# Value products ahead of the transposes in three attentions of a two-block transformer kernel

## The chip, the cores and the metric

The kernel runs on one core of a Trainium2 chip. The metric is the device time of one execution in microseconds (us). Matmuls run on TensorE (PE in the profile; PEld is its weight load), reductions and elementwise work on VectorE (DVE), activations and copies on ScalarE (ACT), a few small operations on GpSimd (POOL); SyncE (SP) issues the transfers. Each engine runs its own instructions in program order and waits for others on semaphores.

## What is computed

The reference runs two transformer blocks one after the other on x of 512 tokens by 1024 features, all in float32. Cut to the attentions:

```python
# block 1
proj = rms_norm(x) @ w_in
# A: 3 groups (window, dilation) = (128, 1), (512, 4), (2048, 16), 4 heads of 64 each
s = q @ k.T * 64 ** -0.5, masked to the window;  m = max(s);  p = exp(s - m);  l = sum(p)
o = (p / l) @ v;  lse = m + log(l);  the groups are weighed with softmax(lse)
# B (latent attention): 8 heads, queries and keys of 96, values of 64, no mask
p = softmax(q @ k.T * 96 ** -0.5);  o = p @ v
h = x + rms_norm(gates * (A @ w_o_a), gates * (B @ w_o_b), ... @ w_out);  h += mlp(h)
# block 2
# four mixers: S5, HGRN2, Fox, mLSTM.  C (Fox): 4 heads of 64, causal
s = q @ k.T * 0.125 + F_q - F_k, masked to k <= q;  p = softmax(s);  o = p @ v
h += rms_norm(mix @ w_out);  h += swiglu(h)
```

## The kernel before

The large products with weights take float32 operands split into a high and a low part and run as three matmuls each (`products`, L237 to L244). Weights come through a ring of three slots: a transfer fills `ring_raw`, ScalarE writes the high half (`split_hi`, L213), VectorE the low half (`split_lo`, L223).

All three attentions are one function, `stage_attention` (L705). It takes a list of tiles (`batches`) of 128 queries of one head:

- A has 24 tiles: 16 of the banded group (one query block against two or three key blocks) and 8 of the dilated ones (four separate 128 x 128 blocks in a tile). Beside it run the products of the two gates: `Beside.pe` issues one or two units of 12 matmuls in every round, directly behind the scores (L663); `Beside.act` adds the gate bias and makes high halves, `Beside.dve` low halves.
- B has 32 tiles, one query block against all 512 keys, and nothing beside it.
- C has 16 tiles, head by head with 1, 2, 3 and 4 key blocks (the causal part). Its scores are three matmul groups: q k, the gate rows (K = 4) and the mask. Beside it `Convolution` (L2211) puts work on VectorE in rounds 0 to 3 and 8 to 11 and four sigmoids on ScalarE in round 5.

The steps of tile i, each with its engine:

1. `scores(i)`, TensorE, L745, into bank i % 2.
2. Row maximum (L827) and `nm` = -scale * maximum (L829), VectorE.
3. `probs` = exp(scores + nm) with its row sum, ScalarE, L803; two buffers.
4. `turn(i)`, TensorE, L757: one transpose for each block of 128 columns, into bank 2 + i % 2. It waits for the exp of its tile (L751).
5. `evac(i)`: copy into `probsT` (L784 to L791, recorded as L629). Even tiles on ScalarE, odd tiles on VectorE.
6. `mix(i)`, TensorE, L769: probsT times the values, one product of 64 columns for each block, into bank 4 + i % 2. It waits for the copy of its tile (L763).
7. Division by the row sum into the output, VectorE, L841 and L844 or L847.

The order on each engine is written out by the loops. In round i ScalarE runs exp(i), then the copy of tile i - 1 if that is even, then the work beside (L795 to L810). VectorE runs the maximum of tile i, then the copy of tile i - 1 if that is odd, then the work beside, then the division of tile i - 2 (L821 to L849). TensorE runs the scores of tile i with the work beside, the transposes of tile i - 1, the value products of tile i - 2 (L774 to L782). At the end of A ScalarE takes the logarithm of the row sums (L814) and VectorE makes 24 subtractions (L854). Each attention is a block of its own: the next stage starts when all engines have ended it.

Of the kernel before, what the change touches and what calls it, by code (L numbers as in the profile page):

```python
# [627 lines left out]
def copy_out(k, who, dst, src):  # L628
    return k.nc.scalar.copy(dst, src) if who == "act" else k.nc.vector.tensor_copy(dst, src)  # L629
# [75 lines left out]
def stage_attention(k, batches, scale, bufs_kb, lse=None, beside=None):  # L705

    nc = k.nc
    nb = len(batches)  # L710
    scored, negmax, expd, turned, ev_act, ev_dve, mixed, out_free = (
        k.sig(n) for n in ("att_scored", "att_negmax", "att_exp", "att_turned", "att_ptT_act", "att_ptT_dve",
                           "att_mixed", "att_out"))
    k.att_n += 1
    probs = k.sb(f"probs{k.att_n}", bufs_kb, [P, 2, 512])
    probsT = k.sb(f"probsT{k.att_n}", bufs_kb + 4, [P, 2, 512])
    ns = max(len(b["segs"]) for b in batches)
    mx = k.sb(f"mx{k.att_n}", bufs_kb + 8, [P, nb, ns])
    nm = k.sb(f"nm{k.att_n}", bufs_kb + 8.5, [P, nb, ns])
    ls = k.sb(f"ls{k.att_n}", bufs_kb + 9, [P, nb, ns])  # L720
    li = k.sb(f"li{k.att_n}", bufs_kb + 9.5, [P, nb, ns])
    chain = k.sig("dve_chain")
    chain_act = k.sig("act_chain")

    def width(b):
        return b["segs"][-1][1]

    with nc.Block() as block:
        @block.sync
        def _(sp):  # L730
            if beside is not None:
                beside.sync(sp)

        @block.tensor
        def _(pe):
            def scores(i):
                b = batches[i]
                if i >= 2:

                    pe.wait_ge(expd.sem, expd.base + i - 1)  # L740
                for (c0, c1), parts in zip(b["segs"], b["scores"]):
                    for m, (a, r, lo, hi, *row) in enumerate(parts):

                        at = dict(tile_position=(row[0], 0)) if row else {}
                        mm = nc.tensor.matmul(k.pb[i % 2][:, lo:hi], a, r, start=m == 0,  # L745
                                              stop=m == len(parts) - 1, skip_group_check=True, **at)
                mm.then_inc(scored.sem, 1)

            def turn(i):
                b = batches[i]  # L750
                pe.wait_ge(expd.sem, expd.base + i + 1)  # L751
                if i >= 2:
                    ev = (ev_act, ev_dve)[i % 2]

                    pe.wait_ge(ev.sem, ev.base + i // 2)
                for c in range(0, width(b), P):
                    mm = nc.tensor.transpose(k.pb[2 + i % 2][:, c:c + P], probs[:, i % 2, c:c + P], k.ident[:, :])  # L757
                mm.then_inc(turned.sem, 1)

            def mix(i):  # L760
                b = batches[i]
                ev = (ev_act, ev_dve)[i % 2]
                pe.wait_ge(ev.sem, ev.base + i // 2 + 1)  # L763
                if i >= 2:

                    pe.wait_ge(out_free.sem, out_free.base + i - 1)
                for n, ((c0, c1), vs) in enumerate(zip(b["segs"], b["values"])):
                    for m, v in enumerate(vs):
                        mm = nc.tensor.matmul(k.pb[4 + i % 2][:, n * DH:(n + 1) * DH],  # L769
                                              probsT[:, i % 2, c0 + m * P:c0 + (m + 1) * P], v,  # L770
                                              start=m == 0, stop=m == len(vs) - 1, skip_group_check=True)
                mm.then_inc(mixed.sem, 1)

            for i in range(nb + 2):  # L774
                if i < nb:
                    scores(i)
                    if beside is not None:
                        beside.pe(pe, i)
                if 1 <= i <= nb:
                    turn(i - 1)  # L780
                if i >= 2:
                    mix(i - 2)  # L782

        def evac(who, eng, i):  # L784
            w = width(batches[i])

            eng.wait_ge(turned.sem, turned.base + i + 1)
            if i >= 2:
                eng.wait_ge(mixed.sem, mixed.base + i - 1)
            copy_out(k, who, probsT[:, i % 2, 0:w], k.pb[2 + i % 2][:, 0:w]).then_inc(  # L790
                (ev_act if who == "act" else ev_dve).sem, 1)  # L791

        @block.scalar
        def _(act):
            for i in range(nb + 1):  # L795
                if i < nb:
                    b = batches[i]
                    act.wait_ge(negmax.sem, negmax.base + i + 1)
                    if i >= 2:

                        act.wait_ge(turned.sem, turned.base + i - 1)
                    for n, (c0, c1) in enumerate(b["segs"]):
                        e = nc.scalar.activation(probs[:, i % 2, c0:c1], k.pb[i % 2][:, c0:c1], ACT.Exp,  # L803
                                                 bias=nm[:, i, n:n + 1], scale=scale,
                                                 accum_out=ls[:, i, n:n + 1])
                    e.then_inc(expd.sem, 1)
                if i >= 1 and (i - 1) % 2 == 0:
                    evac("act", act, i - 1)
                if beside is not None:
                    beside.act(act, i)  # L810
            if lse is not None:

                act.wait_ge(expd.sem, expd.base + nb)
                nc.scalar.activation(mx[:, :, :], ls[:, :, :], ACT.Ln).then_inc(chain_act.sem, 1)  # L814

        @block.vector
        def _(dve):
            link = Chain(dve, chain)
            if lse is not None:
                link(nc.vector.memset(ls[:, :, :], 1.0))  # L820
            for i in range(nb + 2):  # L821
                if i < nb:
                    b = batches[i]
                    m = len(b["segs"])
                    dve.wait_ge(scored.sem, scored.base + i + 1)
                    w = width(b)
                    link(nc.vector.tensor_reduce(  # L827
                        mx[:, i, 0:m], k.pb[i % 2][:, 0:w].rearrange("p (m w) -> p m w", m=m), AX.X, ALU.max))
                    nc.vector.tensor_scalar(nm[:, i, 0:m], mx[:, i, 0:m], -scale, None,  # L829
                                            ALU.mult).then_inc(negmax.sem, 1)  # L830
                if 1 <= i <= nb and (i - 1) % 2 == 1:
                    evac("dve", dve, i - 1)
                if beside is not None and i <= nb:
                    beside.dve(dve, i)
                if i >= 2:
                    j = i - 2
                    b = batches[j]
                    m = len(b["segs"])

                    dve.wait_ge(expd.sem, expd.base + j + 1)  # L840
                    link(nc.vector.reciprocal(li[:, j, 0:m], ls[:, j, 0:m]))  # L841
                    dve.wait_ge(mixed.sem, mixed.base + j + 1)
                    if m == 1:
                        nc.vector.tensor_scalar(b["out"], k.pb[4 + j % 2][:, 0:DH], li[:, j, 0:1], None,  # L844
                                                ALU.mult).then_inc(out_free.sem, 1)
                    else:
                        nc.vector.tensor_tensor(  # L847
                            b["out"], k.pb[4 + j % 2][:, 0:m * DH].rearrange("p (m e) -> p m e", m=m),
                            li[:, j, 0:m].unsqueeze(2).to_broadcast([P, m, DH]), ALU.mult).then_inc(out_free.sem, 1)  # L849
            if lse is not None:  # L850

                dve.wait_ge(chain_act.sem, chain_act.base + 1)
                for dst, i, n in lse:
                    nc.vector.tensor_tensor(dst, mx[:, i, 0:n], nm[:, i, 0:n], ALU.subtract)  # L854
                chain_act.base += 1
    for s in (scored, negmax, expd, turned, mixed, out_free):
        s.base += nb
    ev_act.base += (nb + 1) // 2
    ev_dve.base += nb // 2
    if beside is not None:  # L860
        beside.close()
# [2021 lines left out]
```

## Time and profile before

| | |
|---|---|
| time, median of 3 runs | 1804.71 us (1803.56 to 1804.91) |
| the profiled execution: its time / its span | 1806.47 us / 1804.6 us |
| TensorE busy / weight loads | 1625.3 us (90%) / 1303.4 us (72%) |
| VectorE / ScalarE / GpSimd busy | 827.6 us (46%) / 554.9 us (31%) / 260.4 us (14%) |
| mean granted TensorE clock | 0.911 of 2.4 GHz |
| HBM | 71 GB/s over the span |

The page cuts the span into 40 slices of 45 us; these two lines are the busy tenths of TensorE and its granted clock in tenths of full speed (9 is 90% or more).

```profile
PE   7987999668989899999998999399976899999997
PEclk9998999789999999999998999655568999999999
```

A lies in slices 5 to 8 (185 to 336 us), B in slices 10 and 11 (419 to 494 us), C in slices 27 and 28 (1173 to 1236 us). Matmul lengths in the timeline contain the pipeline's depth, so consecutive matmuls overlap; the distance from one start to the next is the rate. The number in square brackets at the end of a timeline row is the idle time of that engine ahead of it and what ended it.

### The profile page before, as it was taken

To read this page: it belongs to the slowest core of one execution; us is meant where nothing else is said; L and a number is where in the kernel's file an instruction comes from. 1 tells how busy PE (TensorE), PEld (TensorE's weight loads), DVE (VectorE), ACT (ScalarE), POOL (GpSimd) and SP (SyncE) were. 2 spreads that over 40 slices of the span, in tenths; PEclk is the share of its full clock that TensorE was granted. 3 is DMA by queue.
4 is the path that set the end of the run, shared out by engine and by line. 5 is a ranking of instruction groups with operands and counts; after the bars stand their busy time and mean duration, and the time that the engine had idled before them with its cause. 6 is when DMAs were issued, how large, how long until landed. Compare 5 with 4: busy or idle time off the path is not lost. (4 is left out here: it accounts for less than half of the span.)

```text
span 1804.6 us, 18401 instructions
## 1 busy us (share of the span) xinstructions
PE 1625.3 (90%) x7372; PEld 1303.4 (72%) x7372; DVE 827.6 (46%) x1217; ACT 554.9 (31%) x839; POOL 260.4 (14%) x275
## 2 busy tenths in 40 slices
PE   7987999668989899999998999399976899999997
PEld 6875777556767788888876667355775688888886
DVE  4233333456655444443454762463674543323334
ACT  4222333424443422232334212334122422212222
POOL 0000000000022795000011763000220200000000
PEclk9998999789999999999998999655568999999999
DMA  4322121220022222222222211100001123222222
GB/s 165 104 76 73 47 71 36 71 71 1 1 82 77 87 97 105 102 94 93 94 93 79 70 70 66 36 23 1 1 1 53 64 97 107 100 94 94 94 82 94
DMA packets 34633, 129.23 MB, mean 72 GB/s; under 512 B 4548, under 2 KB 18780, under 8 KB 22132
## 3 DMA queue, kind: packets, MB, share of 16 engines
q1 hardware_dynamic: 34260, 127.93, 20.6%
q8 instruction: 58, 0.95, 0.2%
q14 instruction: 27, 0.22, 0.0%
q10 hardware_dynamic: 288, 0.12, 0.0%
HBM read 124.82 MB, written 3.17 MB: 71 GB/s over the span
## 5 line engine op out<-in xcount | busy, mean ns | idle before, releaser
L223 DVE TENSOR_TENSOR ring_lo<-ring_raw,ring_hi 128x2048 fp32r<-128x2048 f32 (+5 forms) x115 | 267.7, 2331 | 246.3 <-ACT ring_hi L213 246.2
L242 PE MATMUL bank<-xT_hi,ring_hi 128*128 128x512 f32 (+1 forms) x864 | 343.7, 398 | 5.1 <-PEq L1257 3.4
L242 PE MATMUL bank<-xT_hi,ring_lo 128*128 128x512 f32 (+1 forms) x864 | 340.0, 393 | 0.0
L242 PE MATMUL bank<-xT_lo,ring_hi 128*128 128x512 f32 (+1 forms) x864 | 339.8, 393 | 0.0
L213 ACT CAST ring_hi<-ring_raw 128x2048 fp32r<-128x2048 f32 (+5 forms) x115 | 213.0, 1854 | 274.7 <-DMA ring_raw<-in_w_ff 130.8
L242 PEld LDWEIGHTS bank<-xT_hi,ring_hi 128*128 128x128 f32 (+1 forms) x864 | 164.0, 190 | 45.1 <-issue 10.0
L242 PEld LDWEIGHTS bank<-xT_hi,ring_lo 128*128 128x128 f32 (+1 forms) x864 | 163.3, 189 | 35.9
L242 PEld LDWEIGHTS bank<-xT_lo,ring_hi 128*128 128x128 f32 (+1 forms) x864 | 163.8, 190 | 34.3
L242 PE MATMUL bank<-ring_hi,hid_hi 128*128 128x512 f32 x432 | 169.9, 393 | 3.8 <-DVE ring_lo L223 3.8
L242 PE MATMUL bank<-ring_lo,hid_hi 128*128 128x512 f32 x432 | 169.4, 392 | 0.0
L242 PE MATMUL bank<-ring_hi,hid_lo 128*128 128x512 f32 x432 | 169.2, 392 | 0.0
L1131 POOL TENSOR_TENSOR stat<-stat 128x1 f32<-128x1 f32 x28 | 18.3, 654 | 700.8 <-DVE stat L1172 700.8
L242 PE MATMUL bank<-ring_hi,xT_hi 128*128 128x512 f32 (+1 forms) x288 | 111.2, 386 | 9.0 <-DVE ring_lo L223 9.0
L242 PE MATMUL bank<-ring_lo,xT_hi 128*128 128x512 f32 (+1 forms) x288 | 110.2, 383 | 0.0
L242 PE MATMUL bank<-ring_hi,xT_lo 128*128 128x512 f32 (+1 forms) x288 | 110.0, 382 | 0.0
L242 PEld LDWEIGHTS bank<-ring_hi,hid_hi 128*128 128x128 f32 x432 | 82.0, 190 | 21.3 <-DVE ring_lo L223 4.2
L803 ACT ACTIVATE probs<-bank,nm 128x128 f32<-128x128 f32 (+3 forms) x96 | 50.3, 528 | 149.1 <-DVE nm L829 149.0
L242 PEld LDWEIGHTS bank<-ring_hi,hid_lo 128*128 128x128 f32 x432 | 81.9, 190 | 17.2
L242 PEld LDWEIGHTS bank<-ring_lo,hid_hi 128*128 128x128 f32 x432 | 81.9, 190 | 17.0
L242 PEld LDWEIGHTS bank<-ring_hi,xT_hi 128*128 128x128 f32 x288 | 58.9, 204 | 21.7 <-issue 6.4
L827 DVE TENSOR_REDUCE mx<-bank 128x1 f32<-128x512 f32 (+4 forms) x72 | 43.3, 601 | 54.3 <-PE bank L745 54.3
L242 PEld LDWEIGHTS bank<-ring_hi,xT_lo 128*128 128x128 f32 x288 | 58.8, 204 | 9.1
(440 smaller groups left out, 2305.1 us busy)
## 6 DMA issues: line engine op xcount, KB each, us to landing
ring_raw<-in_w_ff SPq DMA_DIRECT2D x32, 1024.0 KB, 4.9
ring_raw<-in_w_up SPq DMA_DIRECT2D x22, 1024.0 KB, 4.9
ring_raw<-in_w_proj SPq DMA_DIRECT2D x8, 1024.0 KB, 5.1
ring_raw<-in_w_gates SPq DMA_DIRECT2D x8, 1024.0 KB, 4.9
ring_raw<-in_w_out SPq DMA_DIRECT2D x8, 1024.0 KB, 4.9
ring_raw<-in_w_fm SPq DMA_DIRECT2D x12, 512.0 KB, 4.3
ring_raw<-in_w_dn_a SPq DMA_DIRECT2D x6, 1024.0 KB, 4.9
ring_raw<-in_w_proj SPq DMA_DIRECT2D x8, 512.0 KB, 4.6
```

The source lines that it names most:

```text
L213: k.nc.scalar.copy(k.ring.hi[:, g % SLOTS, 0:n], k.raw[:, g % SLOTS, 0:n]).then_inc(k.w_hi.sem, 1)
L223: k.nc.vector.tensor_tensor(k.ring.lo[:, g % SLOTS, 0:n], k.raw[:, g % SLOTS, 0:n], plain(k.ring.hi[:, g % SLOTS, 0:n]), ALU.subtract).the ...
L242: mm = k.nc.tensor.matmul(out, x, y, start=first and n == 0, stop=last and n == 3 * len(pairs) - 1)
L803: e = nc.scalar.activation(probs[:, i % 2, c0:c1], k.pb[i % 2][:, c0:c1], ACT.Exp, bias=nm[:, i, n:n + 1], scale=scale, accum_out=ls[:, i, ...
L827: link(nc.vector.tensor_reduce(mx[:, i, 0:m], k.pb[i % 2][:, 0:w].rearrange("p (m w) -> p m w", m=m), AX.X, ALU.max))
L1131: g.tensor_tensor(self.rs[:, x:x + 1], self.ms[:, 16 + x:17 + x], self.half, ALU.pow).then_inc(self.root.sem, 1)
```

## The change

Two statements of TensorE's loop change places. In every round TensorE issues the value products of tile i - 2 directly behind the scores of tile i (and the products beside them), and the transposes of tile i - 1 behind those. Each step keeps its own wait. The instructions of all engines are the same in number and kind, and the order on the other engines is not touched. It applies to A, B and C alike.

```diff
                     scores(i)
                     if beside is not None:
                         beside.pe(pe, i)
+                if i >= 2:
+                    mix(i - 2)
                 if 1 <= i <= nb:
                     turn(i - 1)
-                if i >= 2:
-                    mix(i - 2)
```

## Rows read from the trace of the kernel before

**Rows 1.** The page's first part: busy time of each engine.

```profile
PE 1625.3 (90%) x7372; PEld 1303.4 (72%) x7372; DVE 827.6 (46%) x1217; ACT 554.9 (31%) x839; POOL 260.4 (14%) x275
```

**Rows 2.** Stretches: us, busy PE, PEld, DVE, ACT, POOL (x), PEclk, DMA, GB/s.

```profile
185.00:336.00 151.00, 148.55 (x745) 116.18 (x744) 49.34 (x115) 53.55 (x136) 0.00 (x0) 0.98 0.15 53
419.00:494.00 75.00, 72.27 (x461) 54.80 (x462) 48.60 (x146) 33.26 (x82) 0.00 (x0) 1.00 0.01 1
1173.00:1236.00 63.00, 57.55 (x185) 37.62 (x185) 34.57 (x98) 18.05 (x47) 0.00 (x0) 0.54 0.04 17
196.00:199.80 3.80, 3.80 (x18) 3.14 (x17) 0.00 (x0) 0.63 (x2) 0.00 (x0) 1.00 0.00 0
419.00:424.00 5.00, 3.50 (x12) 1.70 (x13) 1.92 (x5) 2.04 (x5) 0.00 (x0) 1.00 0.00 0
294.00:297.00 3.00, 3.00 (x8) 2.32 (x7) 1.76 (x6) 1.22 (x7) 0.00 (x0) 0.50 0.00 0
```

**Rows 3.** Timeline of attention B: start us, length us, engine, line, tiles [idle before].

```profile
429.47 1.08 PE L745 MATMUL bank<-kTb,qTb 96*128 96x512 f32 x2
...
430.39 0.60 PE L757 MATMUL bank<-ident,probs 128*128 128x128 f32 x4
430.59 0.69 DVE L827 TENSOR_REDUCE mx<-bank 128x1 f32<-128x512 f32 x1 [0.31 <-PE bank L745]
...
430.83 1.00 PE L769 MATMUL bank<-vB,probsT 128*128 128x64 f32 x8
...
431.50 0.69 ACT L803 ACTIVATE probs<-bank,nm 128x512 f32<-128x512 f32 x1 [1.41 <-DVE nm L829]
...
431.67 1.08 PE L745 MATMUL bank<-kTb,qTb 96*128 96x512 f32 x2
...
432.09 0.19 ACT L803 ACTIVATION_READ_ACCUMULATOR probs<-bank,nm 128x1 f32 x1
432.18 0.58 ACT L629 COPY probsT<-bank 128x512 f32<-128x512 f32 x1
432.33 0.61 PEld L757 LDWEIGHTS bank<-ident,probs 128*128 128x128 f32 x4 [0.42 <-ACT probs L803]
...
433.58 0.69 DVE L629 COPY probsT<-bank 128x512 f32<-128x512 f32 x1
...
433.86 1.08 PE L745 MATMUL bank<-kTb,qTb 96*128 96x512 f32 x2
...
434.38 0.28 DVE L844 TENSOR_SCALAR oB<-bank,li 128x64 f32<-128x64 f32 x1
```

**Rows 4.** Timeline, the end of attention B.

```profile
486.50 1.08 PE L745 MATMUL bank<-kTb,qTb 96*128 96x512 f32 x2
...
492.01 0.28 DVE L844 TENSOR_SCALAR oB<-bank,li 128x64 f32<-128x64 f32 x1 [0.61 <-PE bank L769]
```

**Rows 5.** Timeline, the end of attention A.

```profile
330.47 0.60 PE L757 MATMUL bank<-ident,probs 128*128 128x128 f32 x4
...
331.11 0.59 ACT L629 COPY probsT<-bank 128x512 f32<-128x512 f32 x1 [3.54 <-PE bank L757]
...
334.25 1.76 DVE L223 TENSOR_TENSOR ring_lo<-ring_raw,ring_hi 128x1536 fp32r<-128x1536 f32 x1 [1.17 <-ACT ring_hi L213]
```

**Rows 6.** Timeline of attention C: round 4, and its last rounds.

```profile
1187.55 0.47 ACT L629 COPY probsT<-bank 128x384 f32<-128x384 f32 x1
1187.70 1.12 PE L757 MATMUL bank<-ident,probs 128*128 128x128 f32 x4 [1.21 <-ACT probs L803]
...
1188.61 1.38 PE L769 MATMUL bank<-tm,probsT 128*128 128x64 f32 x6
...
1230.47 0.47 ACT L629 COPY probsT<-bank 128x384 f32<-128x384 f32 x1
...
1231.53 3.09 PE L769 MATMUL bank<-tm,probsT 128*128 128x64 f32 x14
...
1234.73 0.28 DVE L844 TENSOR_SCALAR ycat<-bank,li 128x64 f32<-128x64 f32 x1 [1.00 <-PE bank L769]
```

## The prediction, made blind

> **What bounds the kernel now.** The first part of the page shows TensorE busy for 1625.3 us of a span of 1804.6 us [rows 1]. The profiled execution took 1806.47 us, so 1.87 us lie around the span. The median of the timed runs is 1804.71 us, 1.76 us below this execution; I make the sum on the execution and then carry it to the median. The table by stretch [rows 2] puts the three attentions at 151, 75 and 63 us, with TensorE busy for 148.6, 72.3 and 57.6 us. They are therefore near TensorE's own rate, but at different clocks: the banded and dilated attention (below A) at 0.98, the latent one (B) at 1.00, that is 2.4 GHz, and Fox (C) at 0.54, nearly all of it 1.2 GHz. In A every round also holds 12 or 24 gate products. B has nothing beside it, C has a convolution on VectorE and ScalarE.
>
> I write S, T, V for the scores, transposes and value products of a tile, and E for the copy of transposed probabilities into probsT. Now TensorE runs S(i), T(i-1), V(i-2); after the change S(i), V(i-2), T(i-1). The same instructions are issued, without a new buffer or a DMA. Two waits change places. T(i-1) waits for exp(i-1), and now gets V's time more. V(i-2) waits for E(i-2), and loses the cover of T(i-1). What counts is where E stands in its engine's order: for even tiles E(i-2) is on ScalarE *behind exp(i-1)*; for odd tiles it is on VectorE and follows T(i-2), which would now end just before S(i).
>
> **B, steady rounds.** The timeline of two rounds [rows 3] gives the period: S of tile 5 (26 rounds before tile 31 at 486.50 [rows 4]) starts at 429.47, S of even tile 6 at 431.67, S of tile 7 at 433.86, so a pair takes 4.39 us. Starts give the parts: S to T 0.92, T to V 0.44, V to S 0.84, sum 2.20 each. TensorE's weight load for T had waited 0.42 us for exp and started at 432.33, 0.05 after the accumulator read ended (432.28); the matmul array itself was hardly idle, as the scores still ran. So exp and TensorE end together now, and the gain to be had in B is small: T takes 0.44 for 512 columns in one go, S has two matmuls of 512, so S alone would need about 0.85 (an estimate) of the 0.92, and no more than 0.07 a round can be won.
>
> Then the odd tile's chain, from S(odd) = 0: reduction at 1.12 (430.59), exp at 2.03 (431.50), accumulator read ends at 2.81, E of the tile before at 2.71 to 3.29 (432.18 + 0.58). Now this E ends behind T and V and nobody notices. After the change V(even) needs it, right behind S(even).
> - V(odd) in the round of S(odd): T(odd) starts 0.44 before S(odd). E on ScalarE follows the start of such a T by 0.64 (330.47 to 331.11 [rows 5]); I take that for VectorE too. E runs 0.20 to 0.89 (0.69 by 433.58). The weight load can start at 0.94. It would anyway have started near 0.7, so the loss is small: V at 1.04 with 0.1 for the first weight load, T(even) at 1.88, S(even) at 2.32.
> - VectorE's bookkeeping behind E (the division starts 0.80 after E, lasts 0.28; the next can start 0.2 after it) ends at 1.20 instead of being long over at 1.12, so reduction, exp and the ScalarE copy come 0.08 later: E(even) ends at 3.37.
> - V(even): 3.37 + 0.05 for the release + 0.1 for the first load = 3.52; + 0.84 for V and 0.44 for T: the next S(odd) at 4.80.
> A pair goes from 4.39 to 4.80, or +0.41. Bounds: with neither first load nor VectorE's delay, 3.29 + 0.05 + 0.84 + 0.44 = 4.62 (+0.23); with 0.25 for the load (432.33 to 432.58) and 0.2 for the delay, 5.07 (+0.68). I take +0.41, since a load that finds the array idle has nothing to wait for, unlike that of 432.33. Rounds 3 to 31 are 14 pairs: **+5.7 us** (3.2 to 9.5). At the start of the stage TensorE waits for exp(0) and exp(1) in both orders, nothing.
>
> **B, its end.** The last S starts at 486.50, the last division at 492.01, 5.51 later [rows 4]. After: V(30) at 3.52, T(31) at 4.36, E(31) on VectorE 5.00 to 5.69, V(31) at 5.84 for 1.00, the division at 6.94: **+1.4 us** (1.2 to 1.7). The cover that is gone is V(30), under which E(31) now runs.
>
> **A.** Between S(i) and V(i-2) lie 12 gate products or more; at full clock 17 of them take 3.8 us [rows 2], so that is at least 2.7 us. E(i-2) hides under them. T(i-1) comes up to 0.84 us later (V's length), and with it, on ScalarE, E, the gate biases and the high halves of the weight ring, on VectorE the low halves; all of these run ahead of TensorE, which is busy for 148.6 of 151 us [rows 2], so nothing until the end. There T(22) starts at 330.47 and E(22) at 331.11; the biases and the high half on ScalarE, then the low half on VectorE (334.25) and its last divisions and subtractions follow in order and end the stage [rows 5]. V(21) now stands ahead of T(22): **+0.84 us** (0, if the chain had slack; 1.7, if TensorE's own end decides, whose E(22) and E(23) are now uncovered). After two rounds of dilated scores the clock drops for over 3 us: in 294 to 297 it was 0.50 [rows 2], that is 1.2 GHz, and half of such a stretch, some 1.7 us, is lost each time. V, T and S remain one run of small products between the same gate products, so I take no change, but one more or fewer of either kind of round may fall: from -3.4 (both gone) to +5.1 (three more).
>
> **C.** At half the clock S takes, by B's 0.85, some 1.7 us for four blocks and 0.85 for two, and has two smaller products behind it; that covers E(odd). E(even) arrives in time in the rounds whose exp is not late. In round 4 it is: E(2) is 1187.55 to 1188.02, T(3) started at 1187.70 after 1.21 us of waiting [rows 6]. V(2) would start at 1188.02 + 0.05 + 0.2 (the first load at half the clock) = 1188.27, with T behind it instead of ahead: **+0.5 us** (0.3 to 0.7; round 2 loses some 0.2 in the same way, which the later exp(3) hides). In rounds 8 and 12 E(even) ends shortly ahead of the scores: 0, at most 0.2 each. At the end V(14) waits for E(14), which ends at 1230.94: V at 1231.2, T(15) 6 products of 0.22 (3.09 / 14) later at 1232.5, E(15) after 0.91 (1187.70 to 1188.61) and 0.2 at 1233.6 to 1234.3, V(15) at 1234.6 for 1.8, the division at 1236.6, against 1234.73: **+1.9 us** (1.5 to 2.2). Sum of C +2.4 (1.8 to 3.3).
>
> **Sum.** 5.7 + 1.4 + 0.84 + 2.4 = 10.3. On the execution 1806.5 + 10.3 = 1816.8; from the median, 1804.7 + 10.3 = **1815.0**.
>
> **Rivals.**
> 1. *The exp wait was the dearer one; faster.* If E(even) could end before S(even) does, B would go at TensorE's own rate, -0.07 x 28 = -2.0, and C would keep the 1.21 of round 4, and with the ends hidden too: 1804.7 - 2.0 - 1.2 = 1801.5, and about 1800.5 with the like in C's round 2. It decides from the point at which E(even) ends before 2.32 + 0.7 = 3.0 after S(odd); the rows put it at 3.29. Speaks for it: TensorE's load does wait for exp in each round. Chance 4%.
> 2. *Only the ends cost.* If a pair in B stays within 0.1 of 4.39, since both waits fall in time that the array uses: 1.4 + 0.84 + 2.4 + 0 to 1.4 = 4.6 to 6, that is 1809 to 1811; with C's also smaller, 1807. Chance 11%.
> 3. *The clock of B falls.* TensorE would be idle 0.4 us of 4.8. At 1.2 GHz a pair takes 2 x 4.27 = 8.5 us, +3.7 over 4.80; all 14 pairs +52 (1867), a few pairs +5 to +20. Against it: in 419 to 424 TensorE was busy for 3.50 of 5.00 us and the clock stayed at 1.00 [rows 2]; for it: C was at 0.50 with TensorE nearly filled. Chance 6%. The Trainium skill, "TensorE: Matmul & The Clock Gate", section "A second HAM failure mode: psum-queue depth-cycling", speaks against this change: short idle gaps between groups of matmuls, it says, made the clock of another kernel swing between its two levels. By that rule B would end at the times of this rival; the row of 419 to 424 has larger gaps at the full level, so the trace does not agree so far.
> 4. *The change does nothing*, as the scheduler of the engine would order the work by itself: TensorE's rows are in the program's order, under 1%, 1804.7.
>
> **How the numbers follow.** My forecast has 78%: 1815.0, and its own terms end at 1808 and 1822 without all extremes together (all low 1807.5, all high 1826). Range 1808 to 1822: it holds most of the forecast and the upper half of rival 2; rival 3 and rival 1 are left out. A measurement can tell about 0.2%, 3.6 us, from no change. Faster 0.03 (rival 1), same 0.07 (the rest of it, 4 and the low part of 2), slower 0.90.
>
> **What would show it.** In B: a pair of S starts 4.80 apart (4.6 to 5.1), TensorE's waits for ACT and DVE copies probsT in place of those for probs, no wait of T for exp; the last division 6.9 behind the last S. In A the same length but 0.8 more behind the last gate product, no waits inside. In C one wait of V(2), a longer end. B unchanged in the steady rounds would make the forecast wrong, as would a granted clock below 1.00 there; A's clock dips could hide some us of either sign.

## The result and the profile after

The changed kernel takes 1817.28 us (median of 4 runs, 1816.4 to 1819.2) against 1804.81 us for the one before (median of 4, 1803.56 to 1808.32): 12.5 us slower, a ratio of 1.007 with a 95% interval of 1.0058 to 1.0082. The profiled execution took 1816.96 us, its span is 1815.2 us, against 1806.47 and 1804.6 before. The forecast was 1815.0 with a range of 1808 to 1822.

The page of after, its busy times and the granted clock in 40 slices:

```profile
PE 1633.3 (90%) x7372; PEld 1299.2 (72%) x7372; DVE 825.2 (45%) x1217; ACT 555.1 (31%) x839; POOL 259.7 (14%) x275
...
PEclk9998999779999999999998999655567999999999
```

TensorE has the same 7372 instructions as in [rows 1], and the busy times of VectorE, ScalarE and GpSimd are within 2.4 us of those before. TensorE's row is 8.0 us longer, but it doesn't tell where: the modelled lengths of its matmuls also cover most of its short waits (67.28 of 68.00 us in B's rounds, shown below), and they grow where the clock is lower. Where the time arose is read by marking the same instruction in both timelines; the difference of the two starts is how far the changed kernel is behind there:

| instruction | before, us | after, us | behind by |
|---|---|---|---|
| A, first scores | 185.8 | 186.1 | +0.3 |
| A, last mask product | 324.9 | 323.1 | -1.7 |
| A, the 24 subtractions | 337.0 | 336.1 | -0.9 |
| B, first scores | 419.6 | 417.2 | -2.4 |
| B, last scores | 486.5 | 489.9 | +3.4 |
| B, last division | 492.0 | 497.7 | +5.7 |
| gate sigmoids, table load behind B | 496.7 | 503.6 | +6.9 |
| C, first scores | 1174.5 | 1181.7 | +7.2 |
| C, last division | 1234.7 | 1245.0 | +10.3 |
| end of the span | 1804.6 | 1815.2 | +10.5 |

B's rounds cost 5.8 us, its end 2.3, the stage behind it 1.2, C 3.1. A came out shorter, because two clock dips of before (one is in [rows 2], 294 to 297; the other, at 0.50 too, lies in 311 to 314) are absent in this execution. Another 1.5 us were won between A's subtractions and B's first scores, in work whose order was not changed.

**B, one pair of rounds.** Timeline of after (start us, length us, engine, line, tiles, idle before and its releaser), to be laid beside [rows 3]:

```profile
427.55 1.02 PE L745 MATMUL bank<-kTb,qTb 96*128 96x512 f32 x2
...
427.75 0.69 DVE L629 COPY probsT<-bank 128x512 f32<-128x512 f32 x1 [0.72 <-PE bank L757]
...
428.50 0.97 PEld L769 LDWEIGHTS bank<-vB,probsT 128*128 128x128 f32 x8 [0.75 <-DVE probsT L629]
...
428.75 0.68 DVE L827 TENSOR_REDUCE mx<-bank 128x1 f32<-128x512 f32 x1
...
429.44 0.61 PE L757 MATMUL bank<-ident,probs 128*128 128x128 f32 x4
...
429.65 0.69 ACT L803 ACTIVATE probs<-bank,nm 128x512 f32<-128x512 f32 x1 [1.80 <-DVE nm L829]
...
429.88 1.02 PE L745 MATMUL bank<-kTb,qTb 96*128 96x512 f32 x2
...
430.33 0.58 ACT L629 COPY probsT<-bank 128x512 f32<-128x512 f32 x1
...
430.96 0.97 PEld L769 LDWEIGHTS bank<-vB,probsT 128*128 128x128 f32 x8 [0.88 <-ACT probsT L629]
...
431.90 0.61 PE L757 MATMUL bank<-ident,probs 128*128 128x128 f32 x4
...
432.35 1.02 PE L745 MATMUL bank<-kTb,qTb 96*128 96x512 f32 x2
```

From the scores of an odd tile at 427.55: VectorE's copy starts 0.20 later, the weight load of the value products 0.95, the next reduction 1.20, the transposes 1.89, exp 2.10, ScalarE's copy ends 3.36 (430.33 + 0.58), the transposes follow at 4.35 and the next odd scores at 4.80. Both value products wait for their copy (0.75 and 0.88 us on the weight-load row), and no transposes of these rounds wait for exp.

**A.** What TensorE waited for between 185 and 337 us (total, times, longest), and the place of the last line:

```profile
PE bank L769 <- DVE probsT L629: 0.8, 1, 0.8
PE bank L745 <- PEq L886: 0.7, 1, 0.7
PE bank L769 <- ACT probsT L629: 0.7, 1, 0.7
PE bank L242 <- ACT gates L1398: 0.4, 1, 0.4
```

```profile
250.28 0.48 ACT L629 COPY probsT<-bank 128x384 f32<-128x384 f32 x1 [3.77 <-PE bank L757]
...
250.65 0.69 ACT L1398 ACTIVATE gates<-bank,cols 128x512 f32<-128x512 f32 x1
...
251.49 0.47 PE L242 MATMUL bank<-xT_hi,ring_hi 128*128 128x512 f32 x1 [0.41 <-ACT gates L1398]
```

The first and third line are the two copies of A's end. The last was not foreseen. The gate bias (L1398) frees the PSUM bank of a gate product. It stands on ScalarE behind the copy, and the copy comes later by the length of the value products. The gate product at 251.49 waited for it 0.41 us and started 0.15 after it ended. By the starts of the rounds, A's rounds 6 and 12 took 0.26 and 0.63 us longer than before.

**B, its end**, in the timeline of after:

```profile
489.88 1.02 PE L745 MATMUL bank<-kTb,qTb 96*128 96x512 f32 x2
...
493.28 1.10 PE L769 MATMUL bank<-vB,probsT 128*128 128x64 f32 x8 [0.91 <-ACT probsT L629]
...
494.87 0.69 DVE L629 COPY probsT<-bank 128x512 f32<-128x512 f32 x1 [2.54 <-PE bank L757]
...
495.62 1.93 PE L769 MATMUL bank<-vB,probsT 128*128 128x64 f32 x8 [0.78 <-DVE probsT L629]
...
497.66 0.28 DVE L844 TENSOR_SCALAR oB<-bank,li 128x64 f32<-128x64 f32 x1 [1.64 <-PE bank L769]
```

The value products of tile 30 wait for ScalarE's copy and those of tile 31 for VectorE's; the last eight take 1.93 us in place of 1.00. The table by stretch (us, busy PE, PEld, DVE, ACT, POOL, granted clock, DMA, GB/s) shows a lower clock there:

```profile
424.00:492.00 68.00, 67.28 (x403) 45.18 (x403) 42.79 (x130) 28.49 (x71) 0.00 (x0) 1.00 0.00 1
492.00:495.00 3.00, 1.92 (x16) 1.44 (x14) 0.43 (x3) 1.23 (x3) 0.00 (x0) 1.00 0.02 5
495.00:498.00 3.00, 1.93 (x8) 1.74 (x8) 1.27 (x5) 0.00 (x0) 0.00 (x0) 0.62 0.00 0
498.00:501.00 3.00, 2.74 (x13) 2.77 (x14) 0.82 (x2) 1.20 (x2) 0.00 (x0) 0.50 0.01 3
```

During the 68 us of B's rounds the clock stays at 1.00 in spite of the gaps. From 492 on TensorE is busy for 1.92 of 3.00 us, and within 495 to 498 the clock falls to 0.50, that is 1.2 GHz. The transposes of the next stage run at that level as well (16 of them take 3.65 us in place of 1.94). The busy share alone does not explain the fall. The kernel before has stretches as empty there, at the full level:

```profile
492.00:495.00 3.00, 1.94 (x16) 1.73 (x16) 1.36 (x3) 1.71 (x4) 0.00 (x0) 1.00 0.01 3
495.00:498.00 3.00, 1.27 (x6) 1.09 (x7) 1.41 (x3) 1.66 (x3) 0.00 (x0) 1.00 0.00 0
```

### The profile page after: what moved, and what is told of

It reads as the page before. It is cut to its first block and busy times, and to the rows that moved or that the text cites. A ratio compares the mean times of both kernels' runs of the same rounds, so it can differ in the third digit from the quotient of the medians.

```text
span 1815.2 us, 18401 instructions
## 1 busy us (share of the span) xinstructions
PE 1633.3 (90%) x7372; PEld 1299.2 (72%) x7372; DVE 825.2 (45%) x1217; ACT 555.1 (31%) x839; POOL 259.7 (14%) x275
```

## The experiments

All comparisons are with the kernel before, run beside each kernel on the same chip; 1 permille is 1.8 us. Where one difference in us is given with a ratio, it is worked out from the ratio. What is read from a trace is read from one execution.

### One attention at a time

```diff
+                early = k.att_n in (1,)      # A; (2,) for B, (3,) for C
+                if early and i >= 2:
+                    mix(i - 2)
                 if 1 <= i <= nb:
                     turn(i - 1)
-                if i >= 2:
+                if not early and i >= 2:
                     mix(i - 2)
```

A alone:

> The changed order in A alone, B and C as before. Account of the prediction, mended by the trace of after: the copies, and the gate biases behind them on ScalarE, come later by the length of the value products, and TensorE waits for a gate bank in two rounds (0.3 and 0.6 us) and ends 0.9 later: +1.8 us, less or more by 1.7 for each clock dip that comes or goes (the profiled execution of before had two, that of after none), so the median between -1.5 and +3. Rival (the loss of the whole change is spread over all three attentions by the lost cover): +4, a third of 12.5.

Measured: 1807.14 against 1804.46 us, ratio 1.0013 (1.0005 to 1.0022), +2.3 us. From A's first scores to its last mask product it took 137.1 us, against 136.0 in the C-alone kernel, which has the old order in A and no clock dip there either; from there to the subtractions 13.0 against 12.1. So A costs 1.1 us in its rounds and 0.9 at its end. That these add up to nearly the +2.3 is no proof, for more moved in this execution where the order is as before: against the C-alone kernel 1.3 us were won between A and B, and 2.8 were lost between C and the end of the span.

B alone:

> The changed order in B alone. Account of the prediction: the pair of rounds takes 4.79 instead of 4.39 us, 14 pairs, +5.7; end of the stage +1.4 to +2.3; the transposes behind it at a lower clock up to +1.2: +8 to +9 us in all. Rival (spread evenly): +4.

Measured: 1815.91 us, ratio 1.0061 (1.0047 to 1.0075), +11.0 us: more than expected. In its trace B is 7.5 us longer from the first scores to the last division, the stage behind it 1.2, and the products behind that another 1.5, for the clock is at 0.50 until past 506 us.

C alone:

> The changed order in C alone. Account of the prediction: +2.4 to +3 us, of which 0.5 in round 4 and 1.9 at the end. Rival (spread evenly): +4; rival (C is limited by TensorE at the low clock, the order plays no part): 0.

Measured: 1807.93 us, ratio 1.0017 (1.0008 to 1.0026), +3.1 us, and 3.1 us from C's first scores to its last division in the trace. TensorE's waits in C:

```profile
PE bank L769 <- ACT probsT L629: 3.7, 3, 1.8
...
PE bank L769 <- DVE probsT L629: 0.8, 1, 0.8
```

That is the start, round 4 and the end. But the rounds between, in which nothing waits, were each 0.10 to 0.11 us longer than before, ten times in a row. First a round of C alone, then the same round of the kernel before:

```profile
1220.94 1.91 PE L769 MATMUL bank<-tm,probsT 128*128 128x64 f32 x8
...
1222.65 0.42 PE L757 MATMUL bank<-ident,probs 128*128 128x128 f32 x1
...
1222.99 0.50 PEld L745 LDWEIGHTS bank<-fm 64*128 64x128 f32 x2 [0.22 <-issue]
```

```profile
1220.73 0.42 PE L757 MATMUL bank<-ident,probs 128*128 128x128 f32 x1
...
1220.94 1.81 PE L769 MATMUL bank<-tm,probsT 128*128 128x64 f32 x8
...
1222.68 0.50 PEld L745 LDWEIGHTS bank<-fm 64*128 64x128 f32 x2
```

The scores' first weight load now stands behind the transposes, and the row shows it 0.22 us idle ("issue": it waited for nothing in the profile); it comes 0.34 us after the transposes' start. Before, the value products followed a one-block transpose by 0.21, and the scores' load came behind the value products without idle time ahead of it. So in C the order costs a little by itself.

Taken one at a time the three come to 16.4 us, together the change costs 12.5. The sum of three such intervals is wide (some 4 us), and the clock took another course behind the stages from kernel to kernel; the runs don't settle how the difference of 3.9 us divides between the two.

### Is it the copy's place behind exp?

The changed order in B alone, and on ScalarE:

```diff
             for i in range(nb + 1):
+                if k.att_n == 2 and i >= 1 and (i - 1) % 2 == 0:
+                    evac("act", act, i - 1)
                 if i < nb:
...
-                if i >= 1 and (i - 1) % 2 == 0:
+                if k.att_n != 2 and i >= 1 and (i - 1) % 2 == 0:
                     evac("act", act, i - 1)
```

> The changed order in B alone, and there ScalarE copies the even tile before the exp of the next instead of behind it. Account of the prediction (the copy is late because it stands behind exp): the copy ends 0.84 after the scores start, a pair takes 2.33 + 2.22 = 4.55 instead of 4.79, 3.4 us less than with the changed order alone, about +3.5 to +4.5 against before. Rival (what is lost is the cover of the transposes, wherever the copy stands): pair 4.79, the same time as with the changed order alone.

Measured: 1812.9 against 1804.46 us, ratio 1.0041 (1.0028 to 1.0054), +7.4 by the ratio and +8.4 by the medians: 3.0 (medians) to 3.6 us (ratios) less than B alone. The timeline:

```profile
440.93 1.02 PE L745 MATMUL bank<-kTb,qTb 96*128 96x512 f32 x2
...
441.13 0.59 ACT L629 COPY probsT<-bank 128x512 f32<-128x512 f32 x1 [2.00 <-PE bank L757]
441.61 0.69 ACT L808 ACTIVATE probs<-bank,nm 128x512 f32<-128x512 f32 x1
441.76 0.97 PEld L769 LDWEIGHTS bank<-vB,probsT 128*128 128x128 f32 x8 [0.64 <-ACT probsT L629]
...
442.90 0.69 ACT L808 ACTIVATE probs<-bank,nm 128x512 f32<-128x512 f32 x1 [0.51 <-DVE nm L834]
...
443.15 1.02 PE L745 MATMUL bank<-kTb,qTb 96*128 96x512 f32 x2
...
444.10 0.97 PEld L769 LDWEIGHTS bank<-vB,probsT 128*128 128x128 f32 x8 [0.75 <-DVE probsT L629]
```

The copy starts 0.20 after the scores instead of 2.78 behind those of the odd tile, with exp behind it. The weight load of the value products starts 0.83 after the scores in this round and 0.95 in the other; the starts of the scores (440.93, 443.15, 445.48) make a pair of 4.55, as worked out. The rival's 4.79 is out. About 60% of the steady loss (0.25 of 0.41 a pair) is the place of ScalarE's copy behind exp; the rest is that a copy right behind its transposes has only the scores as cover (with a whole round of cover, in the version without the waits below, no such wait is left). The level was above the expectation again, as with B alone. In the trace 3.0 us lie behind B's last division, where the clock was at 0.50 for some 10 us.

### What B's end costs

```diff
-                early = k.att_n in (2,)              # B alone
+                early = k.att_n == 2 and i < nb       # b_old_end: rounds 2 to 31 only
+                early = k.att_n == 2 and i >= nb      # b_new_end: round 32 only
```

> The changed order in B alone and only in its rounds 2 to 31; in round 32 the transposes of tile 31 stand ahead of the value products of tile 30, as before. Theory: of the 11.5 us that the changed order in B alone costs, 5.7 are the steady rounds and the rest comes from the end, where TensorE waits twice for a copy and its clock then falls to 1.2 GHz and stays there for 6 to 10 us. So here +5.5 to +6.5 us, and the clock at 1.00 up to 20 us behind the last division. Rival (the clock falls because of the idle gaps in all rounds of B): the clock falls here as well, +9 or more.

Measured: 1811.02 against 1805.1 us, ratio 1.0035 (1.0023 to 1.0048), +5.9 by the medians and +6.3 by the ratio. In the trace B is 5.8 us longer from first scores to last division, and behind it (last division at 495.5) the clock stays up:

```profile
492.00:495.00 3.00, 2.56 (x22) 2.27 (x21) 1.48 (x7) 1.25 (x3) 0.00 (x0) 1.00 0.02 5
495.00:498.00 3.00, 2.28 (x20) 2.02 (x19) 0.85 (x2) 1.19 (x3) 0.00 (x0) 1.00 0.01 3
498.00:501.00 3.00, 0.84 (x4) 0.67 (x4) 1.92 (x4) 1.67 (x3) 0.00 (x0) 1.00 0.00 0
```

> The converse: B as before up to round 31, and only in round 32 the value products of tile 30 ahead of the transposes of tile 31. Theory: about +1.5 by the two uncovered copies and another +2 to +4 by the clock behind them: +3.5 to +5.5 us, the granted clock at 0.5 within 3 us of the last division. Rival (idle gaps in all rounds of B bring the clock down): +1.5, clock at 1.00.

Measured: 1808.61 us, ratio 1.0019 (1.001 to 1.0028), +3.5 by the medians and +3.4 by the ratio, with B's rounds as before. Here the last division is at 493.4; the clock falls about 2 us ahead of it and returns nearly 7 us later:

```profile
489.00:492.00 3.00, 2.22 (x15) 1.98 (x16) 1.11 (x4) 0.00 (x0) 0.00 (x0) 0.85 0.00 0
492.00:495.00 3.00, 2.28 (x11) 2.12 (x12) 0.28 (x1) 0.00 (x0) 0.00 (x0) 0.50 0.00 0
495.00:498.00 3.00, 2.64 (x13) 2.24 (x11) 1.93 (x3) 2.11 (x4) 0.00 (x0) 0.52 0.01 3
498.00:501.00 3.00, 1.68 (x7) 1.43 (x8) 0.84 (x2) 1.98 (x3) 0.00 (x0) 1.00 0.00 0
```

In the trace 2.2 us are lost up to the last division and another 1.2 in the stage behind it. The two runs add up to 9.7 of B's 11.0 us by the ratios, 9.4 of 11.5 by the medians. One instruction group moved in one round of 34 costs more than a quarter of the change (3.5 of 12.5; the interval of the 3.5 is 1.8 to 5.1). The rival, that the idle gaps in all rounds bring the clock down, is out as far as one traced execution can tell: they are all there in the first of these kernels, and the clock did not fall.

### A version without the waits

```diff
+                lag = 3 if k.att_n in (2, 3) else 2
+                if lag == 3 and 3 <= i:
+                    mix(i - 3)
                 if 1 <= i <= nb:
                     turn(i - 1)
-                if i >= 2:
+                if lag == 2 and 2 <= i < nb + 2:
                     mix(i - 2)
...
-                if i >= 2:
-                    j = i - 2
+                if i >= lag:
+                    j = i - lag
```

with one round more in the loops of TensorE and VectorE.

> In B and C the value products of THREE tiles back stand directly behind the scores and ahead of the transposes of the last tile, and VectorE divides tile i - 3 in round i; A as before. The same buffers. Account of the prediction: each copy has a whole round of cover and exp has that of the value products, so no wait is left in the steady rounds of B: a pair takes 4.27 to 4.30 instead of 4.39, -1.5 us; C wins 0.5 of round 4's wait; the ends cost nothing. 1802.5 against 1804.5, which lies at the edge of what can be told. Rival (putting the value products behind the scores costs by itself, as 64-column products cannot hide the next weight load): +2 to +6.

Measured: 1807.99 against 1805.1 us, ratio 1.0017 (1.0008 to 1.0026), +2.9 by the medians and +3.1 by the ratio: a miss in sign. The mechanism was right in B, where the value products of two rounds apart start

```profile
440.17 1.00 PE L769 MATMUL bank<-vB,probsT 128*128 128x64 f32 x8
...
444.46 1.00 PE L769 MATMUL bank<-vB,probsT 128*128 128x64 f32 x8
```

so a pair takes 4.29 us, and from first scores to last division 1.7 us are won. But the clock fell within 495 to 501 us, and the 1.7 us were gone by C. C was 0.7 us longer. And 2.6 us more were lost between C's last division and the end of the span, where the clock was at 0.50 for longer (on average 0.70 in 1370 to 1380 us against 1.00 before). With B alone in this order:

> Value products of three tiles back directly behind the scores in B alone; A and C as before. With B and C both so, the profiled execution won 1.6 us from B's first scores to its last division (pair 4.29 instead of 4.39), and the whole kernel still came out 2.9 us slower. Theory: part of that was C, where value products behind the scores cost 0.1 us in each round by themselves, and part the granted clock behind B and behind C, which falls at other places when the stages ahead take another time. So here B is 1.6 shorter again and the kernel between 1802.5 and 1806. Rival (the order in B itself hurts what follows, by the clock behind it): 1807 or more.

Measured: 1804.64 against 1804.21 us, ratio 1.0003 (0.9994 to 1.0012): no difference. In the trace B won 1.7 us again, the clock averaged 0.67 and 0.76 in 492 to 495 and 495 to 498, and at C's first scores the kernel was as far ahead as at B's. B's own gain is paid back behind it.

This also limits what the end of B shows. TensorE's one wait there is 0.34 us in this kernel, and yet the clock fell. Where it fell in the traces sorts the kernels into three. In the four with the changed order in B's last round (after, B alone, the copy ahead of exp, the end alone) it fell 0.6 to 2.3 us ahead of the last division. In the two with value products of three tiles back it fell 5 us behind it. In four with the old order there it did not fall (before, C alone, the old end, and the kernel with the gate bias first, told below). But in the fifth of these, A alone, it fell 6 us behind the last division, with the same instructions in B and behind it as in the kernel before (the row of 498 to 501 in its trace):

```profile
498.00:501.00 3.00, 3.00 (x8) 2.31 (x7) 1.22 (x2) 3.00 (x7) 0.00 (x0) 0.50 0.01 3
```

So a fall in the stages behind B needs no change in B. The early fall came with the changed last round in each of four traces and in none of the other seven; what in that order brings it, and whether it needs the waits for the copies, stays open.

### The gate bank in A

The order of A changed, and on ScalarE:

```diff
+                if k.att_n == 1:
+                    beside.act(act, i)
                 if i >= 1 and (i - 1) % 2 == 0:
                     evac("act", act, i - 1)
-                if beside is not None:
+                if beside is not None and k.att_n != 1:
                     beside.act(act, i)
```

> The changed order in A alone, and there ScalarE does the gate biases and the high halves of the ring ahead of the copy of the even tile. Theory: in the changed order TensorE waits for a gate bank in two rounds because the bias that frees it stands behind a later copy; with the bias first these two waits (0.3 and 0.6 us) go, A's first 16 rounds are 0.9 shorter than with the changed order alone. The end may be some us longer, since the last copy now stands behind a high half. Rival (the gate bank is late for another reason): the waits stay.

Measured: 1804.05 against 1805.1 us, ratio 0.9995 (0.9987 to 1.0004): no difference from the kernel before. TensorE's waits in A are now

```profile
PE bank L769 <- DVE probsT L629: 0.8, 1, 0.8
...
PE bank L769 <- ACT probsT L629: 0.7, 1, 0.7
```

with no line for the gates, and first scores to last mask product take 136.2 us, against 137.1 with the changed order alone. That is the expected 0.9, and within 0.2 of what the old order takes without clock dips (136.0). The end of A, which might have been longer, took 12.7 us against 13.0. By the ratios the kernel is 3.2 us faster than A alone, and only 1.2 of that lie in A; the rest is not explained. It is the best kernel that has the changed order anywhere, and it doesn't beat the one before by what can be told.

## Why the prediction was right, and where it was off

The sign, the mechanism and the range held; the time was 2.3 us (of 12.5) short. On the profiled execution the forecast was 1816.8 and the measured time 1816.96, and that close hit is luck. The terms named below cost some 14.3 us in that trace, 4.0 more than the 10.3 of the sum. The absent dips of A (3.2) and the 1.5 us between A and B hid this.

- **B's rounds** (predicted +5.7, pair 4.80): the pair is 4.80, and the 14 pairs cost 5.7; round 2 adds 0.1. 66.9 us from the scores of tile 0 to those of tile 31 became 72.7, +5.8, and the same with the old end. The steps lie within 0.03 us of those worked out, with one exception in which two errors cancel: the value products started with their weight load (0.95 and 3.41 after the odd scores, not 1.04 and 3.52) and then took 0.94 to the transposes and not 0.84. That the copy's place behind exp matters was tested by moving it.
- **B's end** (predicted +1.4): 2.3 us in after, 2.2 when the end alone is changed. The two waits for copies came (0.91 and 0.78 us); the step that failed is the full clock that the term assumed: the eight products of tile 31 took 1.93 in place of 1.00.
- **Behind B** (predicted nothing): 1.2 us in after; up to C's first scores 2.7 when B alone was changed, 1.3 with only the end changed. This is the largest missing term. The prediction weighed the clock as a rival for B's rounds, where the gaps are, and did not price it for the end, where TensorE waits twice within 3 us and a stage with idle time follows.
- **A** (predicted +0.84): the end was 0.9. The rounds cost 1.1 us more, 0.9 of it in the two rounds in which a gate bank comes late. The prediction named the biases behind the later copy and took the slack of the ring for theirs. The dips, left at no change with a range, moved in the profiled execution by about -3.2 us. No link to the order is shown: of the eight traced kernels with the old order in A three have both dips (before, the copy ahead of exp, three tiles back in B and C) and five have none, and the three with the changed order have none.
- **C** (predicted +2.4): 3.1. The scores behind round 4 came 0.46 us later than before against the first scores, as predicted (0.5), with the loss of round 2 hidden in it. The rounds without a wait, which had been put at nothing, cost 0.1 each, 1.1 from round 5 on. The rest, 1.5, is the end (1.9 predicted).
- **The rivals.** The exp wait did vanish and brought nothing that can be seen, as E(even) ended at 3.36 and not before 3.0; what it is worth once the copies are covered is 0.10 a pair (4.39 to 4.29, the version without the waits). "Only the ends" is out by the 5.8 of the rounds, and "does nothing" by the interval of the ratio. The clock never fell in B's rounds, so the pattern of short gaps of which the Trainium skill tells ("TensorE: Matmul & The Clock Gate", "A second HAM failure mode: psum-queue depth-cycling") did not appear at gaps of 0.75 and 0.88 us on the weight-load row of a 4.80 us pair. The falls that came lie at the end of the stage or behind it.

## What to carry to other kernels

When a consumer is moved closer to its producer, look up where the copy between them stands in its own engine's queue: a copy behind another tile's exp ends only after that exp and all that it waits for, and the things queued behind the copy (here a bias that frees a bank) become late with it. Price the end of a stage apart from its rounds, with the clock: a wait that is harmless in a full pipeline stands in the drain beside other idle time, and here the stage behind it ran at half the clock. And a gain of one or two us in one stage should be followed to the end of the kernel before it is believed, for a clock dip elsewhere can come or go with it.

## What the runs showed of the hardware that was not expected

- The clock held at 1.00 through 68 us in which TensorE's weight-load row shows idle gaps of 0.75 to 0.88 us in each round, and fell right behind a stretch with 1.92 of 3.00 us busy. After that it stayed at 0.50 for nearly 7 us (after, end alone) and some 10 us (B alone). In the kernel before, stretches with 1.94 and 1.27 of 3.00 us busy at the same place left it at 1.00.
- With the same order in A, the profiled execution had two dips in A in three kernels and none in five others, worth 3.2 us together. In the three, A's first scores started at 185.5 to 185.8 us; in all traces without dips they started at 186.1 us or later. A single profiled execution can't give an effect of that size in such a kernel.
- At 1.2 GHz the scores' first weight load came 0.34 us behind the start of a one-block transpose, and no idle time was shown for it behind a longer run of value products; the order of three groups, all ready, changed a round by 0.1 us.
